# Hybrid decoder step on one Trainium2 core: the six whole-attention heads handled in pairs on TensorE

## What is computed

```python
s_own = jnp.einsum('bqhd,bqkhd->bqhk', q, ko) * scale + bias
s_own = jnp.where(d_own >= 0, s_own, -jnp.inf)
p, _ = softmax_lse(jnp.concatenate([s_sel, s_own], axis=-1))
return einsum(p_sel, vs) + einsum(p_own, vo)
```

## Time and profile before

| | |
|---|---|
| median of 3 runs | 1091.47 us (1091.17 to 1091.48) |
| span of the profiled execution, first to last instruction | 1089.3 us |
| PE busy | 1067.3 us, 98% |
| DVE, ACT, POOL busy | 505.0, 338.0, 77.5 us |
| chain that ended last, by engine | PE 94%, DVE 3% |
| stretch with the whole attention (297 to 391.7 us) | 94.70 us |
| stretch with the sample attention (391.7 to 505.65 us) | 113.95 us |

### The profile page before, as it was taken

The page is one execution under the profiler, slowest core; times in us unless marked ns, Lnnn a source line. Parts: engine busy times, 40 slices in busy tenths (PEclk is TensorE's granted clock), DMA queues, the critical chain, the costliest instruction groups (busy, mean ns, idle before and its releaser), DMA issues.

```text
span 1089.3 us, 18518 instructions
## 1 busy us (share of the span) xinstructions
PE 1067.3 (98%) x7750; PEld 962.8 (88%) x7750; DVE 505.0 (46%) x887; ACT 338.0 (31%) x557; POOL 77.5 (7%) x90
## 2 busy tenths in 40 slices
PE   5999999999999999999999999999999999999998
PEld 4798899877877775678999999999999999999997
DVE  6624447454466631215453655554545554432232
ACT  5433223323344423412222234332322222322222
POOL 4000013001110010001120300000000000000000
PEclk8999999999999999999999999999999999999999
DMA  8483344411120055341223222322232223223202
GB/s 256 97 300 116 43 137 83 156 47 63 60 82 24 22 157 170 95 138 39 78 92 103 79 79 78 102 92 78 78 113 82 78 78 116 70 68 107 78 30 82
DMA packets 104554, 104.76 MB, mean 96 GB/s; under 512 B 10697, under 2 KB 101251, under 8 KB 104231
## 3 DMA queue, kind: packets, MB, share of 16 engines
q1 hardware_dynamic: 101384, 92.92, 27.8%
q0 software_dynamic: 3088, 10.67, 3.2%
HBM read 97.76 MB, written 14.88 MB: 103 GB/s over the span
## 4 chain that ended last, share of the span: by engine, by line
PE 94%; DVE 3%; issue 1%; POOL 1%; ACT 0%; DMA 0%; SPq 0%; DVEq 0%; POOLq 0%; ACTq 0%
PE acc L459 75%; PE acc L927 3%; PE acc L947 3%; PE acc L1017 2%; PE acc L1060 2%; PE acc L937 1%; PE acc L846 1%; PE acc L1002 1%; PE acc L856 1%; PE acc L813 1%; DVE h_lo L1873 1%; POOL mt L767 1%; PE acc L1135 1%; DVE w_lo L443 0%; DVE h_hi L1865 0%
## 5 line engine op out<-in xcount | busy, mean ns | idle before, releaser
L459 PE MATMUL acc<-h_hi,w_hi 128*128 128x256 f32 (+1 forms) x1520 | 468.9, 308 | 8.1 <-DVE w_lo L443 4.9
L459 PE MATMUL acc<-h_lo,w_hi 128*128 128x256 f32 (+1 forms) x1520 | 440.2, 290 | 0.0
L459 PE MATMUL acc<-h_hi,w_lo 128*128 128x256 f32 (+1 forms) x1520 | 438.3, 288 | 0.0
L459 PEld LDWEIGHTS acc<-h_hi,w_hi 128*128 128x128 f32 x1520 | 287.5, 189 | 69.4 <-issue 57.4
L459 PEld LDWEIGHTS acc<-h_hi,w_lo 128*128 128x128 f32 x1520 | 288.7, 190 | 0.0
L459 PEld LDWEIGHTS acc<-h_lo,w_hi 128*128 128x128 f32 x1520 | 288.6, 190 | 0.1
L438 ACT ACTIVATE w_hi<-raw 128x1024 fp32r<-128x1024 f32 x135 | 141.3, 1046 | 432.8 <-PE acc L459 432.1
L443 DVE TENSOR_TENSOR w_lo<-raw,w_hi 128x1024 fp32r<-128x1024 f32 x135 | 166.4, 1232 | 109.0 <-ACT w_hi L438 103.6
L459 PE MATMUL acc<-s_hi,w_hi 128*128 128x256 f32 (+1 forms) x352 | 101.6, 288 | 0.0
L459 PE MATMUL acc<-s_lo,w_hi 128*128 128x256 f32 (+1 forms) x352 | 101.3, 288 | 0.0
L459 PE MATMUL acc<-s_hi,w_lo 128*128 128x256 f32 (+1 forms) x352 | 100.7, 286 | 0.0
(11 more groups left out here) (299 smaller groups left out, 1198.7 us busy)
## 6 DMA issues: line engine op xcount, KB each, us to landing
raw<-in_w_in SPq DMA_DIRECT2D x25, 1024.0 KB, 5.2
raw<-in_w_gate_up SPq DMA_DIRECT2D x22, 1024.0 KB, 5.0
raw<-in_w_down SPq DMA_DIRECT2D x8, 1024.0 KB, 5.3
ring<-in_cache_dsa_kv SPq DMA_DIRECT2D x4, 1024.0 KB, 7.2
raw<-in_w_out SPq DMA_DIRECT2D x4, 1024.0 KB, 5.4
out<-in_cache_dsa_kv SPq DMA_DIRECT2D x2, 2016.0 KB
rev<-tab POOLq DMA_DIRECT2D x1, 3840.0 KB, 35.8
ring<-in_cache_moba_k SPq DMA_DIRECT2D x48, 64.0 KB, 1.9
```

Of the source, the lines that this page charges most:

```text
L459: ins = nc.tensor.matmul(acc[:, bank, 0:HALF[half]], a[:, k, :], two(b[:, kx + k, :], half), start=first and k == k0 and c == 0, stop=last ...
```

## The change

The 24 units are taken in pairs, an even head and the next odd one of the same query tile. TensorE's order per half block becomes: scores of both, six products, outputs of both (of the pair two before), twelve products, transposes of both (of the pair before), six products. The transposes of odd units go to bank 2 instead of 6. ACT's order becomes exps(u), turned(u - 2), exps(u + 1), turned(u - 1). DVE collects both outputs with one copy over 128 partitions (`collect_two`). The sample attention is moved later by a quarter of a block (T_SA = 33.25), and gets three more waits (SP for v_stored, TensorE for pt_ev and, in `turn_p`, for tok_done).

```diff
-        T_SA = 33
+        T_SA = 33.25
+        def turned_bank(u):
+            return 2 if u > ND and (u - ND) % 2 else 6
...
+                            sp.wait_ge(sem("v_stored"), 32 * 6)
...
-                    if n >= 1:
-                        pe.wait_ge(sem("pt_ev"), n)
+                    if u < ND + 2:
+                        if n >= 1:
+                            pe.wait_ge(sem("pt_ev"), n - max(u - ND, 0))
+                    else:
+                        pe.wait_ge(sem("pt_ev"), n - 1)
+                    if u == ND + 1:
+                        pe.wait_ge(sem("tok_done"), 2 * len(turns))
...
-                        pe.wait_ge(sem("o_ev"), n)
+                        pe.wait_ge(sem("o_ev"), n - max(u - ND, 0) % 2)
...
-                    for c in range(NU - ND + 3):
-                        u = ND + c
+                    for u in range(ND, NU + 4, 2):
                         if u < NU:
                             yield unit_time(u, 0)
                             scores(unit_segs[u][0])
-                        if 3 <= c:
-                            yield unit_time(u, 0.25)
+                            scores(unit_segs[u + 1][0])
+                        if u >= ND + 4:
+                            yield unit_time(u, 0.5)
+                            outputs(unit_segs[u - 4][0])
                             outputs(unit_segs[u - 3][0])
-                        if 2 <= c < NU - ND + 2:
-                            yield unit_time(u, 0.75)
+                        if ND + 2 <= u < NU + 2:
+                            yield unit_time(u, 1.3)
                             turn_p(unit_segs[u - 2][0])
+                            turn_p(unit_segs[u - 1][0])
...
+                    pe.wait_ge(sem("pt_ev"), len(segs))
...
+                    for u in range(ND, NU + 2, 2):
+                        if u < NU:
                             yield unit_time(u, 0.6)
                             exps(u)
+                        if u >= ND + 2:
+                            yield unit_time(u, 1.45)
+                            turned(unit_segs[u - 2][0])
+                        if u < NU:
+                            yield unit_time(u, 1.6)
+                            exps(u + 1)
+                        if u >= ND + 2:
+                            yield unit_time(u, 1.75)
+                            turned(unit_segs[u - 1][0])
...
+                def collect_two(n):
+                    _, i, h, k0, off = segs[n]
+                    dve.wait_ge(sem("o_mm"), n + 2)
+                    nc.vector.tensor_copy(qT[:, 2 + h // 2, P * i:P * (i + 1)], acc[:, 7, 0:P]).then_inc(sem("o_ev"), 2)
...
+                    for u in range(ND, NU + 4):
+                        if u < NU:
                             yield unit_time(u, 0.3)
                             biased(u)
-                        if 3 <= c:
-                            yield unit_time(u, 0.5)
-                            collect(unit_segs[u - 3][0])
-                        if 1 <= c < NU - ND + 1:
+                        if ND + 1 <= u < NU + 1:
                             yield unit_time(u, 0.6)
                             normal(u - 1)
+                        if u >= ND + 4 and (u - ND) % 2 == 0:
+                            yield unit_time(u, 0.9)
+                            collect_two(unit_segs[u - 4][0])
```

More of the change, by code:

```diff
@@ L932, in turn_p @@
                     pe.wait_ge(sem("p_done"), u + 1)
-                    if n >= 1:
-                        pe.wait_ge(sem("pt_ev"), n)
+                    if u < ND + 2:
[5 more added lines that the diff above has]
+                        pe.wait_ge(sem("tok_done"), 2 * len(turns))
                     src = scores_in(u)
                     for k in range(i + 1 - k0):
-                        ins = nc.tensor.transpose(acc[:, 6, P * k:P * (k + 1)], src[:, off + P * k:off + P * (k + 1)], ident)
+                        ins = nc.tensor.transpose(acc[:, turned_bank(u), P * k:P * (k + 1)], src[:, off + P * k:off + P * (k + 1)], ident)
                     ins.then_inc(sem("pt_tr"), 1)
@@ L1246, in turned @@
                     w = P * (i + 1 - k0)
-                    nc.scalar.copy(PTs[:, n % 2, 0:w], acc[:, 6, 0:w]).then_inc(sem("pt_ev"), 1)
+                    nc.scalar.copy(PTs[:, n % 2, 0:w], acc[:, turned_bank(u), 0:w]).then_inc(sem("pt_ev"), 1)
                 def attention():
@@ L1259, in attention @@
                                 exps(u)
-                    for c in range(NU - ND + 3):
-                        u = ND + c
-                        if 3 <= c:
-                            yield unit_time(u, 0.1)
-                            turned(unit_segs[u - 3][0])
-                        if c < NU - ND:
+                    for u in range(ND, NU + 2, 2):
+                        if u < NU:
                             yield unit_time(u, 0.6)
                             exps(u)
+                        if u >= ND + 2:
[7 more added lines that the diff above has]
+                            turned(unit_segs[u - 1][0])
                 def gates():
```

## The result

The changed kernel takes **1074.0 us** (median of 4 runs, 1072.73 to 1075.76), beside 1091.32 us (1091.16 to 1091.48) for the kernel before on the same chip: a ratio of 0.9842, with a 95% interval of 0.9828 to 0.9856. The profiled execution took 1075.07 us, its span 1073.3. The forecast was 1080.1 with a range of 1077.5 to 1086.5: the direction was right, the gain was 17.3 us and not 11.4, and the time lies outside the range.

A forecast was written before the change was run, and what follows sets the result against it. The prediction took TensorE's own queue to be the bound. Its terms, -8.8 - 4.5 - 0.6 + 2.5 = -11.4 us, took 1091.47 to 1080.1 us, with a range of 1077.5 to 1086.5.

The forecast's parts named there:

- What bounds the kernel, and how it was costed: TensorE's own queue sets the time, not clock or idle; insertions, costed from starts: scores 22.4 us, outputs 21.3.
- Shared passage: Scores and outputs: two heads share one passage from whole-array products to half-array matmuls and back; -8.8 us.
- Overlap inside the pair: Head B's first record runs beside A's second in scores (-3.2 us), beside A's last in outputs (-1.3); -4.5 us.
- The wait at 384.37: TensorE's 0.58 us wait for DVE, with sample preparations queued ahead of a collect, goes away; -0.6 us.
- Handover: Last sample transposes wait 3.0 us as four y_lo precede DVE's Osb copy; a block 39 wait goes; net +2.5 us.
- Transposes, DVE, added waits: Transposes keep count and cost, DVE has room for its copies, the three new semaphore waits are ready; no cost.
- Rival 1: Scores and outputs: the pair shares the passage but nothing overlaps; 1084.6 us, chance 0.27.
- rival 2: Scores and outputs: the two heads run fully side by side; 1071.5 us, chance 0.06.
- Rival 3: Scores and outputs: going to the other half costs the full passage; 1093.4 us, chance 0.07.
- Rival 4: Second outputs of each pair wait for the PTs copy, DVE and ACT setting the pace; 1094.9 us, chance 0.06.

The follow-up runs named there:

- e3: Changed kernel with the odd head's scores reading the same rows (partitions 0 to 63) as the even head's; 1081.69 us.
- e7: Changed kernel with the odd head's outputs going to the same 64 PSUM partitions as the even head's, in other columns; 1080.47 us, single run.
- e4: Kernel before the change with only T_SA moved from 33 to 33.25; 1095.77 us, ratio 1.0033 to the kernel before.
- e1: Changed kernel with T_SA set back from 33.25 to 33; 1071.27 us.
- e6: Changed kernel run again without any edit, five more runs; 1074.78 us.
- e8: Changed kernel with the outputs of a pair alternating between heads in steps of two key tiles; 1072.07 us, single run.
- e2: Changed kernel with the outputs of a pair alternating between heads key tile by key tile; 1074.13 us.

## Why the prediction was right and wrong

**What bounds the kernel, and how it was costed: right.** TensorE's queue set the time, and the cost of an insertion, counted from starts, gave every price to 0.02 us. But its first paragraph also said that the clock was not at stake, and that held for the kernel before only.

**Shared passage, -8.8: right.** e3 and e7 measure it on one half, without overlap: 0.40 and 0.34 us once per pair. For two halves the table shows it: a pair of scores costs what one head did, passage included. This is the Trainium skill's "TensorEngine Tiling (Array Packing)", Key Properties (a change of mode drains, a change of tile does not), and the runs agree as far as the price goes; that the passage is a drain, none of them can show.

**Overlap inside the pair, -4.5: the step that failed.** The prediction said that B's first record may start with A's second, since the queue holds A's two first. It took the order in the queue for the order of the starts. The counts show B's first record starting with A's first in the scores, and in the outputs with four key tiles 3.5 record steps before its turn. Measured: scores 6.4 us of overlap (all 30 x 0.213) instead of 3.2, outputs 4.2 instead of 1.3, together 10.6 for 4.5. The reading of the Trainium skill's "TensorE: Matmul & The Clock Gate", Part 3, on which it leaned (matmuls start and end in program order), did not hold in these records; the Trainium skill's "TensorEngine Tiling (Array Packing)", Theoretical Speedup, with its twofold, came out for the scores and, interleaved, for the outputs. The error was one of weights too: no row spoke on this step, its two ends were 0 and 13, and full overlap got 0.06 and stayed out of the range.

**The wait at 384.37, -0.6: right in size**, though by the pairs and not by the move, since e4 kept it; e1, with the pairs alone, has 0.2 us at the transposes in its place.

**Handover, +2.5: mechanism and wait right, its price too low.** The wait was 2.88 us for 3.0, and the 0.49 us came back (0.75 by starts): +2.1. Missed: the clock after it, +1.5 in this execution.

**Transposes, DVE, added waits, at nothing: right.** PE waited for no PTs in any pair.

The terms as measured: -11.1 for the scores (22.3 to 11.2), -8.2 for the outputs (21.2 to 13.0), -0.6, +2.9, -0.75, +1.5, together -16.3 us; the spans differ by 16.0 (1089.3 and 1073.3), with 0.2 us lost before block 27 and 0.3 behind block 132. The median gained 17.3, since two of the four executions took 1072.8, 2.3 less than the profiled one. The clock at the handover, the start-up and the end can each make that much, and which did was not settled.

**Rivals.** Rival 1 has the passage right and fell on the overlap; rival 2 (1071.5) is true of the scores and in part of the outputs: with 2.4 us for what the outputs did not overlap (13.0 less 10.6) and 1.2 for a handover of 3.7 instead of 2.5, it gives 1075.1, what the profiled execution took; that it agrees to the tenth is luck. Rival 3 fell to the table, in which the second head adds no passage. Rival 4 fell: no wait for PTs.

## What to carry to other kernels

Put float32 matmuls of two heads that use different halves of the array directly behind one another, and alternate them matmul by matmul: in this kernel two then cost what one did, while blocks of six or eight records per head overlapped by only some 3.5. When a stage's due time moves, compare the order on the engines that it depends on, not only on its own; a quarter block put four operations ahead of the one copy that TensorE waited for. And price a wait of a few us on TensorE with what the clock may take behind it: 1.5 to 2.9 us here, for a wait of 2.88.

## What the runs showed that was not expected

- Records of different halves do not start in the order of the queue: B's first started with A's first in the scores, and the early start reached about four records (1.28 us behind four, 1.71 us behind eight, 1.23 us alternating).
- The weight loads of both heads fall together too: all four records of the pair of scores at 354.27 are loaded within 0.30 us.
- A single wait of 2.88 us, in a stream that else runs at the 2.4 GHz level, brought the 1.2 GHz level in all seven profiles that have it. In the changed kernel it came 1.7 us after the wait, for 3.4 us (489.2 to 492.6); in e6, e3, e7 and e8 it came 0.3 to 1.5 us after it and lasted as long. In e2 and e4 it came within the wait and went on for 6.6 and 5.7 us after it. Measured losses are 1.5 us in the changed kernel, 2.5 in e4 and 2.9 in e2. Why it comes sooner or later, and whether an execution with the wait can keep the clock, stays open.
